# The four big projections by Strassen's seven block products, on eight cores of a Trainium2

## The chip, the cores and the metric

One program runs on all eight NeuronCores of a Trainium2 chip, each on its own 1024 tokens (four sequences of 2048, two cores to a sequence). The metric is the device time of the slowest core in microseconds. No core talks to another.

## The reference

One block of a streaming encoder, on activations of width 2048:

```python
h = rmsnorm(x, norm1_g)
b_a, c_a, v_a, v_b, g_a, g_b = split(h @ w_in)     # 1024 x4, 2048 x2 columns
u   = causal_depthwise_conv3(c_a * v_a)
y_a = (b_a * u) @ w_a_out
y_b = pool_scale * per_group_linear(trailing_mean(v_b, 2/4/8/16) - v_b)
x   = x + (sigmoid(g_a + b) * y_a + sigmoid(g_b + b) * y_b) @ w_o
h2  = rmsnorm(x, norm2_g)
x   = x + (silu(h2 @ w_gate) * (h2 @ w_up)) @ w_down   # width 5632
out = rmsnorm(x, final_g)
```

## The kernel before, in words

Five engines run one program text each; `Emitter.op` issues an instruction on its engine in program order and puts in front of it the semaphore waits that its tiles need. Nothing is reordered, so an instruction that waits holds all behind it on its engine.

Weights come from DRAM in f32 and are cast to bf16 on the way by POOL's queue, in jobs, into the four slots of `wring` (`issue_job`, L297 to L311). A slot's next job is issued when TensorE is done with it, so three jobs are always ahead. All matmuls go through `mm_group` (L406): a chain of 128x128 stationary blocks, each with 512 moving columns, into one PSUM bank.

- Start: nine row tiles of x are loaded by SP; for each, `norm_stats` (ScalarE Square and Sqrt, L367), `norm_to_T` (VectorE reciprocal and scaling L383, TensorE transposes L394, evacuation L399 or L402) give h transposed in `hT`. Tiles 5 to 8 are transposed in between the first groups of `mixA`. Matmuls on zeros (`warm`) keep TensorE busy meanwhile.
- Convolution branch, j = 0 to 7: 16 halo columns, then per half of the tokens (512 columns) three groups of 16 matmuls; `mixA_ew_blk` combines.
- Pooling branch, j = 0 to 7: two groups of 16; running sums L569, then L575.
- Gates, j = 0 to 15, per half: 16 + 8 + 16 + 2 matmuls into four banks; sigmoids L611 and L614, products L617, L619, L622, into `mg`.
- Output projection: 4 column blocks of 512 x 8 token tiles x 16 matmuls, added into the residual `x1`, which lies in SBUF in f32 (L665). In the last column block the second norm of tile i follows at once, and the transposed result takes the place of `mg`.
- FFN: 4 groups of 11 hidden blocks. Gate/up: per block and half 16 + 16 matmuls, Silu L694, product L696. Down: 4 column blocks x 8 token tiles x 11 matmuls, added into `x1` (L753). In the last group the final norm follows each tile (`final_norm`, L724), then SP stores it. The first gate/up group of the FFN runs on the first token half while the second half is still being normed.

Of the kernel before, what the change touches and what calls it, by code (L numbers as in the profile page):

```python
# [1 line left out]

# [5 lines left out]
F32 = mybir.dt.float32  # L8
# [6 lines left out]
D = 2048  # L15
KD = 16
T = 1024
# [5 lines left out]
G = 4  # L23
FG = NF // G
SLOT = 6144
NSLOT = 4
EPS = 1e-6
POOL_W = (2, 4, 8, 16)

JOB_SIZES = ([6144] * 8 + [6144, 6144, 4096] + [5376] * 16 + [4096] * 8  # L30
             + ([4096] * FG + [FG * 512] * 4) * G)
WTOTAL = sum(JOB_SIZES)

def pack_weights(inputs):
# [9 lines left out]
    def kv(a):  # L44
        return a.reshape(a.shape[0] // 128, 128, a.shape[1]).transpose(1, 0, 2)

    blocks = []
    for j in range(8):
        blocks.append(np.stack([kv(w_in[:, wi * 1024 + j * 128:wi * 1024 + (j + 1) * 128]) for wi in range(3)],
                               axis=1).reshape(128, -1))  # L50
    for q in range(3):
        n = 3 if q < 2 else 2
        blocks.append(kv(w_in[:, 3072 + q * 384:3072 + q * 384 + n * 128]).reshape(128, -1))
    for j in range(16):
        g = j // 4
        blocks.append(np.concatenate([
            np.stack([kv(w_in[:, 4096 + j * 128:4096 + (j + 1) * 128]),
                      kv(w_in[:, 6144 + j * 128:6144 + (j + 1) * 128])], axis=2).reshape(128, -1),
            kv(w_a_out[:, j * 128:(j + 1) * 128]).reshape(128, -1),
            kv(w_pool[g * 256:(g + 1) * 256, (j % 4) * 128:(j % 4 + 1) * 128]).reshape(128, -1)], axis=1))  # L60
    for db in range(4):
        for hh in range(2):
            blocks.append(kv(w_o[hh * 1024:(hh + 1) * 1024, db * 512:(db + 1) * 512]).reshape(128, -1))
    for gi in range(G):
        for fi in range(FG):
            fidx = gi * FG + fi
            blocks.append(np.concatenate([kv(w_gate[:, fidx * 128:(fidx + 1) * 128]).reshape(128, -1),
                                          kv(w_up[:, fidx * 128:(fidx + 1) * 128]).reshape(128, -1)], axis=1))
        for db in range(4):
            blocks.append(kv(w_down[gi * FG * 128:(gi + 1) * FG * 128, db * 512:(db + 1) * 512]).reshape(128, -1))  # L70
# [8 lines left out]
class Res:  # L79
    def __init__(self, name):  # L80
        self.name = name
        self.reset()
# [762 lines left out]
```

How the kernel before makes its waits and increments, by code:

```python
    def wait_tokens(self, engname, toks):  # L118
        if self.cur != engname:
            return
        need = {}
        for (s, v) in toks:
            if need.get(s, 0) < v:
                need[s] = v
        for s, v in need.items():
            if self.waited.get(s, 0) >= v:
                continue
            self.eng.wait_ge(s.h, v)
            self.waited[s] = v
# [1 line left out]
    def op(self, engname, fn, reads=(), writes=(), sem=None, inc=1):  # L131
        toks = []
        for r in reads:
            toks += r.w
        for w in writes:
            toks += w.w + w.r + w.pr
        self.wait_tokens(engname, toks)
        ins = fn(self.eng) if self.cur == engname else None
        s = sem if sem is not None else self.engsem[engname]
        s.count += inc
        if ins is not None:
            ins.then_inc(s.h, inc)
        tok = (s, s.count)
        for r in reads:
            r.r.append(tok)
        for w in writes:
            if w.r:
                w.pr = w.r
                w.r = []
                w.w = [tok]
            else:
                w.w.append(tok)
        return tok
```

## Time and profile before

| | |
|---|---|
| runs (three) | 1609.62, 1611.08, 1611.22 us; median 1611.08 |
| span of the profiled execution, slowest core | 1608.6 us (the page gives no other time for it); the cores 1606.4 to 1608.6 |
| mean granted TensorE clock by core | 0.991 to 0.994 |
| instructions | 19498 |
| busy | TensorE 1567.9, VectorE 396.1, ScalarE 211.5, POOL 51.8 us |
| HBM | 252.89 MB read, 8.39 MB written |

The span runs from a core's first to its last instruction; the runs' times hold 2.5 us more. PE stands for TensorE's matmuls, PEld for its weight loads, DVE for VectorE, ACT for ScalarE, POOL for GpSimd, SP for SyncE, with q for a queue; L696 is a line of the kernel. A row of windows has the stretch and its length, then busy time and instructions of PE, PEld, DVE, ACT, POOL, the granted clock as a share of 2.4 GHz, the busy share of the 16 DMA engines and GB/s. A busy TensorE isn't one at its peak, since its records overlap: the step from one matmul to the next has to be read from the starts of groups. POOL's 51.8 us are the issuing of DMAs.

### The profile page before, as it was taken

To read this page: it belongs to the slowest core of one execution; us is meant where nothing else is said; L and a number is where in the kernel's file an instruction comes from. 1 tells how busy PE (TensorE), PEld (TensorE's weight loads), DVE (VectorE), ACT (ScalarE), POOL (GpSimd) and SP (SyncE) were. 2 spreads that over 40 slices of the span, in tenths; PEclk is the share of its full clock that TensorE was granted. 3 is DMA by queue.
4 is the path that set the end of the run, shared out by engine and by line. 5 is a ranking of instruction groups with operands and counts; after the bars stand their busy time and mean duration, and the time that the engine had idled before them with its cause. 6 is when DMAs were issued, how large, how long until landed. Compare 5 with 4: busy or idle time off the path is not lost.

```text
span 1608.6 us, 19498 instructions; the slowest of 8 cores (1606.4 to 1608.6 us)
## 1 busy us (share of the span) xinstructions
PE 1567.9 (97%) x7655; PEld 725.1 (45%) x7805; DVE 396.1 (25%) x527; ACT 211.5 (13%) x330; POOL 51.8 (3%) x102
## 2 busy tenths in 40 slices
PE   5999999999999999999999999999999999999997
PEld 2444444444444444544444444444444444444443
DVE  4422236222222212621012211022111022110126
ACT  5311112111111100510000000000000000000004
POOL 0000000000000000000000000000000000000000
PEclk8999999999999999999999999999999999999999
DMA  9863325444454385374464344453444543444615
GB/s 264 157 119 66 67 49 85 81 76 69 71 84 79 53 239 102 53 131 78 73 102 73 56 79 74 84 92 53 79 79 73 94 83 53 79 77 73 103 24 209
DMA packets 18215, 146.14 MB, mean 91 GB/s; under 512 B 2160, under 2 KB 2240, under 8 KB 2624
## 3 DMA queue, kind: packets, MB, share of 16 engines
q0 software_dynamic: 13968, 116.40, 43.1%
q1 hardware_dynamic: 4160, 28.49, 5.1%
q8 instruction: 65, 1.06, 0.3%
q14 instruction: 22, 0.18, 0.0%
HBM read 252.89 MB, written 8.39 MB: 162 GB/s over the span
## 4 chain that ended last, share of the span: by engine, by line
PE 96%; DMA 2%; issue 1%; DVE 1%; ACT 1%; SPq 0%; POOL 0%; DVEq 0%; ACTq 0%; POOLq 0%
PE ps L409 95%; DMA wring<-wpack 1%; DMA arenaC<-x_c 1%; PE ps L394 1%; ACT arenaC L368 0%; DVE arenaC L383 0%; DVE arenaB L724 0%; ACT arenaA L399 0%; DVE arenaB L402 0%; DVE arenaA L402 0%; ACT L373 0%; SPq L418 0%; DVE arenaA L753 0%; DVE arenaA L665 0%; ACT arenaC L614 0%
## 5 line engine op out<-in xcount | busy, mean ns | idle before, releaser
L409 PE MATMUL ps<-arenaB,wring 128*128 128x512 bf16 x2759 | 605.6, 379 | 4.5 <-DVE arenaB L402 1.5
L409 PE MATMUL ps<-arenaA,wring 128*128 128x512 bf16 (+1 forms) x2700 | 520.7, 351 | 8.2 <-DMA wring<-wpack 4.5
L409 PEld LDWEIGHTS ps<-arenaB,wring 128*128 128x128 bf16 x2816 | 275.3, 98 | 333.5 <-issue 1.6
L409 PEld LDWEIGHTS ps<-arenaA,wring 128*128 128x128 bf16 x2752 | 241.6, 98 | 286.7 <-issue 9.2
L409 PE MATMUL ps<-wring,arenaC 128*128 128x512 bf16 x1380 | 303.1, 379 | 1.5
L409 PEld LDWEIGHTS ps<-wring,arenaC 128*128 128x128 bf16 x1408 | 137.7, 98 | 166.2
L696 DVE TENSOR_TENSOR arenaC<-ps,arenaC 128x512 bf16<-128x512 f32 x88 | 60.9, 692 | 541.5 <-PE ps L409 539.7
L694 ACT ACTIVATE arenaC<-ps 128x512 f32<-128x512 f32 x88 | 52.5, 597 | 772.9 <-PE ps L409 772.9
L753 DVE TENSOR_TENSOR arenaA<-ps,arenaA 128x512 f32<-128x512 f32 x128 | 88.5, 691 | 200.3 <-PE ps L409 193.5
L409 PE MATMUL ps<-wring,arenaB 128*128 128x512 bf16 x501 | 110.4, 379 | 0.6
L309 POOL DMA_DIRECT2D wring<-wpack x94 | 49.6, 529 | 1430.6 <-PE ps L409 1430.6
L409 PEld LDWEIGHTS ps<-wring,arenaB 128*128 128x128 bf16 x512 | 49.8, 98 | 59.3
L368 ACT ACTIVATE arenaC<-arenaA 128x2048 bf16<-128x2048 f32 x18 | 34.4, 1909 | 153.0 <-DVE arenaA L665 86.8
L619 DVE SCALAR_TENSOR_TENSOR arenaC<-ps,prm,arenaC 128x512 f32<-128x512 f32 x32 | 24.0, 751 | 108.9 <-ACT arenaC L614 108.5
L617 DVE TENSOR_TENSOR arenaC<-ps,arenaC 128x512 f32<-128x512 f32 x32 | 22.1, 691 | 103.5 <-PE ps L409 103.5
L614 ACT ACTIVATE arenaC<-ps,prm 128x512 f32<-128x512 f32 x32 | 22.0, 687 | 142.5 <-PE ps L409 142.5
L665 DVE TENSOR_TENSOR arenaA<-ps,arenaA 128x512 f32<-128x512 f32 x32 | 21.6, 689 | 75.1 <-DMA arenaA<-x_c 38.4
L611 ACT ACTIVATE arenaC<-ps,prm 128x512 f32<-128x512 f32 x32 | 22.0, 687 | 100.3 <-PE ps L409 100.3
L488 DVE TENSOR_TENSOR arenaC<-ps,arenaC 128x512 f32<-128x512 f32 x16 | 11.1, 692 | 93.2 <-PE ps L409 92.4
L569 DVE TENSOR_TENSOR arenaC<-arenaC 128x1039 f32<-128x1039 f32 (+3 forms) x20 | 24.8, 1238 | 26.8 <-ACT arenaC L561 25.5
L394 PE MATMUL ps<-identb,arenaC 128*128 128x128 bf16 (+1 forms) x272 | 17.9, 221 | 12.4 <-DVE arenaC L383 10.8
L495 DVE SCALAR_TENSOR_TENSOR arenaC<-arenaC,prm 128x512 f32<-128x512 f32 x32 | 24.0, 752 | 18.2 <-ACT arenaC L491 16.2
(48 smaller groups left out, 243.0 us busy)
## 6 DMA issues: line engine op xcount, KB each, us to landing
wring<-wpack POOLq DMA_DIRECT2D x53, 1024.0 KB, 9.6
wring<-wpack POOLq DMA_DIRECT2D x16, 1408.0 KB, 12.1
wring<-wpack POOLq DMA_DIRECT2D x16, 1344.0 KB, 11.9
wring<-wpack POOLq DMA_DIRECT2D x9, 1536.0 KB, 13.9
arenaA<-x_c SPq DMA_DIRECT2D x10, 1024.0 KB, 25.8
out<-arenaB SPq DMA_DIRECT2D x8, 1024.0 KB, 3.9
arenaB<-x_c SPq DMA_DIRECT2D x4, 1024.0 KB, 23.2
arenaC<-norm_g SPq DMA_DIRECT2D x2, 1024.0 KB, 13.4
```

Of the source, the lines that this page charges most:

```text
L309: em.op("pool", lambda e, s=s, sz=sz, off=off: e.dma_start(out=slot(s, sz), in_=wpack[:, off:off + sz]), writes=[r_slot[s]], sem=s_w[s], i ...
L368: em.op("act", lambda e: e.activation(out=sq[0:npart, :], in_=src_ap, func=AF.Square, accum_out=ssb[0:npart, col:col + 1]), reads=src_res, ...
L394: ins = e.transpose(pt[:, k, 0:npart], hbuf[0:npart, k * 128:(k + 1) * 128], identb[0:npart, 0:npart])
L409: ins = e.matmul(out_ap, lhs_fn(k), rhs_fn(k), start=(k == 0), stop=(k == nk - 1))
L495: em.op("dve", lambda e, sh=sh, pc=pc: e.scalar_tensor_tensor(out=R3[:, o0:o0 + 512], in0=R2[:, c0 - sh:c0 - sh + 512], scalar=PW(pc), in1 ...
L569: em.op("dve", lambda e, dst=dst, cur=cur, lo=lo, sh=sh: e.tensor_tensor(out=dst[:, lo:TT], in0=cur[:, lo:TT], in1=cur[:, lo - sh:TT - sh] ...
L611: em.op("act", lambda e, b0=b0, par=par, j=j: e.activation(out=sga[par], in_=bank(b0), func=AF.Sigmoid, bias=PW(j)), reads=[r_bank[b0], R[ ...
L617: em.op("dve", lambda e, b0=b0, par=par: e.tensor_tensor(out=m1, in0=bank(b0 + 1), in1=sga[par], op=ALU.mult), reads=[r_bank[b0 + 1], r_sg ...
L619: em.op("dve", lambda e, b0=b0, par=par, j=j: e.scalar_tensor_tensor(out=m2, in0=bank(b0 + 3), scalar=PW(64 + j), in1=sgb[par], op0=ALU.mu ...
L694: em.op("act", lambda e: e.activation(out=sg[par], in_=bank(bg), func=AF.Silu), reads=[r_bank[bg]], writes=[r_sg[par]])
L696: em.op("dve", lambda e: e.tensor_tensor(out=act[:, fi, o0:o0 + 512], in0=bank(bu_), in1=sg[par], op=ALU.mult), reads=[r_bank[bu_], r_sg[p ...
L753: em.op("dve", lambda e, b=b, i=i, db=db: e.tensor_tensor(out=x1[:, i, db * 512:(db + 1) * 512], in0=bank(b), in1=x1[:, i, db * 512:(db + ...
```

## The change

With X cut in four blocks along rows and contraction and W along contraction and columns, the product is built from seven block products in place of eight. The blocks of a unit are 1024 of the contraction by 128 weight columns by 512 tokens (projections with weights stationary), or 128 tokens by 512 columns (activations stationary: output and down projection). Five sums of weight blocks and five of activation blocks are used, all bf16 in SBUF, made by VectorE.

`run_group` emits the seven products one after another, with lists of follow-up work (`urg`, by product) and a queue of other VectorE work (`pump`) spread between; what belongs to the last product is handed on as `carry` and is emitted behind the next unit's first product. Banks X, Y, Z of two parities are used.

```diff
+            def run_group(prods, urg, carry, extra=None):
+                for s in range(7):
+                    prods[s]()
+                    if extra and s in extra:
+                        extra[s]()
+                    for c in (carry if s == 0 else urg.get(s - 1, [])):
+                        c()
+                    pump(-(-len(queue) // (7 - s)))
+                return urg.get(6, [])
...
+            def common(par, X, Y, Z, need_e=True):
+                urg = {
+                    0: [lambda: acopy(tS[par], bank(X), [r_bank[X]], [r_tS[par]])],
+                    1: [lambda: tt(tD[par], bank(Y), tS[par], ALU.subtract, [r_bank[Y], r_tS[par]], [r_tD[par]])],
+                    2: [lambda: tt(tE[par], bank(Z), tD[par], ALU.add, [r_bank[Z], r_tD[par]], [r_tE[par]])],
+                    3: [], 4: [lambda: tt(tE[par], tE[par], bank(Y), ALU.subtract, [r_tE[par], r_bank[Y]], [r_tE[par]])],
+                    5: [], 6: [],
+                }
+                return urg
...
+                spec = [(X, "s5", "22", True), (Y, "22", "s4", True), (Z, "s1", "s1", True), (X, "11", "s3", False),
+                        (Y, "s2", "11", False), (Z, "s7", "s7", False), (X, "s6", "s6", False)]
```

`c11` adds bank Z and tD after product 5, `c22` adds bank X and tE after product 6; C12 and C21 are read straight from banks X and Y. `prep_w` queues a unit's five weight sums (`ASPEC`: 1024 elements a partition each), `prep2` those of a gate/up unit or, for a down unit, five (chunk 0) or ten; both are called one unit ahead.

In-projection: 32 units of 4096 weight columns (two output blocks of 128 each): 8 of C and v (`cv`), 4 of B, 4 of v_b, 16 of gates. The first two `cv` are done plainly, with 16-matmul groups (`std_mm`), before the block sums of h are complete:

```diff
+            n1(5)
+            n1(6)
...
+            halo_mm(19, 2)
+            std_mm(19, "1", 0, 0)
+            std_mm(19, "2", 0, 1)
+            n1T(5, 2, "dve")
+            n1(7)
...
+            n1T(6, 3, "dve")
+            n1(8)
+            for s_ in range(1):
+                for spec in BSPEC:
+                    bsum(spec, 0, H4, H4, r_Hr, r_Hr)
+            halo_mm(20, 3)
+            n1T(7, 2, "dve")
+            n1T(8, 3, "dve")
...
+            halo_cv(2, 0)
+            std_ew(0, 0, 0, 1)
+            std_mm(20, "1", 0, 2)
```

(`n1` is statistics and scaling of a tile, `n1T` its transposes and evacuation, `bsum` a sum of 2048 elements.) Then the other 14 of the first 16 units follow, with the running sums of the pooling (`pool_tail`) and the convolution (`conv_tail`) put on the queue. In the gate units the 8 + 2 matmuls per half of the mixer of unit j - 1 stand behind products 1 to 4 of unit j.

Output projection: two halves of 1024 columns (dp), four groups (tp) of token tiles tp and tp + 4, products of 8 matmuls. The sums of W_o (`w_sum`, 4096 elements) and of merged (`mo_sum`, 1024) of the first group are emitted at the start:

```diff
+            mo_sum(AS["s5"], 0)
+            w_sum(BS["s4"], W0, r_w0, W0s, r_w0)
+            mo_sum(AS["s1"], 0)
+            w_sum(BS["s1"], W0, r_w0, W0s, r_w0)
+            for f_ in (lambda: w_sum(BS["s3"], W0, r_w0, W0s, r_w0), lambda: mo_sum(AS["s2"], 0),
+                       lambda: mo_sum(AS["s7"], 0), lambda: w_sum(BS["s7"], W0, r_w0, W0s, r_w0),
+                       lambda: mo_sum(AS["s6"], 0), lambda: w_sum(BS["s6"], W0, r_w0, W0s, r_w0)):
+                f_()
...
+                    if dp == 1:
+                        urg[6].append(lambda tp=tp: norm2_stage1(tp))
+                        if tp > 0:
+                            o = tp - 1
+                            extra = {3: lambda o=o: norm2_tr(o, o), 5: lambda o=o: norm2_tr(o, o + 4)}
+                            urg[0].append(lambda o=o: norm2_scale(o, o))
+                            urg[2].append(lambda o=o: norm2_scale(o, o + 4))
+                            for spec in BSPEC:
+                                urg[5].append(lambda o=o, spec=spec: norm2_sums(o, spec))
...
+            ffn_begin2()
+            prep2(units[0])
+            pump(100)
+            norm2_scale(3, 3)
+            norm2_tr(3, 3)
+            norm2_scale(3, 7)
+            norm2_tr(3, 7)
+            for spec in BSPEC:
+                norm2_sums(3, spec)
```

`norm2_stage1` also stores the residual to a DRAM scratch `x1_d` (SP, 16 stores of 0.5 MB), since its SBUF space goes to the FFN. FFN: chunks of 4, 8, 8, 8, 8, 8 hidden blocks, `CHUNKS`. Weight loads go through four slots; a down unit (one dp of one chunk, products of 2 or 4 matmuls, four groups) takes two of them:

```diff
+            for c in range(NCH):
+                if c + 1 < NCH:
+                    units.append(("ff", c + 1, 0))
+                for dp in range(2):
+                    units.append(("dn", c, dp))
+                if c + 1 < NCH:
+                    for f in range(1, CHUNKS[c + 1]):
+                        units.append(("ff", c + 1, f))
...
+                    b = raw2[n_ % 4]
+                    load(key, bb(b, JOFF[key][1]), r_slot[b], s_slot[12 + n_ % 4])
...
+                    carry = run_group(prods, urg, carry)
+                    issue2(1)
+                    continue
...
+                if ui in hostq:
+                    prep2(hostq[ui])
...
+                        urg[3].append(lambda X=X, i0=i0: acopy(st(i0)[:, 512:1024], bank(X), [r_bank[X]], [r_st[i0]]))
...
+                        def accum(i, t, dp=dp):
+                            return lambda: em.op("pool", lambda e: e.dma_start(
+                                out=x1_d[t * 128:(t + 1) * 128, dp * 1024:(dp + 1) * 1024],
+                                in_=fb(STB[i], 1024, (i % 2) * 1024), accum_op=ALU.add), reads=[r_st[i]],
+                                writes=[r_x1d[t][dp]], sem=s_st[i], inc=16)
+                        urg[5].append(accum(i0, t1))
+                        urg[6].append(accum(i1, t2))
...
+                    left = 4 - tp
+                    keep = list(queue)
+                    queue.clear()
+                    take = -(-len(keep) // left)
+                    queue.extend(keep[:take])
+                    rest = keep[take:]
+                    carry = run_group(prods, urg, carry)
+                    queue.extend(rest)
+                pump(100)
+                issue2(2)
```

So the down results of chunks 0 to 4 are staged in four SBUF buffers (`st`) and added to the scratch by DMAs from POOL's queue. For the last chunk the scratch is read back into SBUF by SP (16 loads of 0.5 MB), six additions per group go there (two of them on GpSimd), and in its second unit the final norms of tiles tp and tp + 4 are handed on in `carry` behind each group.

## Rows read from the trace of the kernel before

**Rows 1.** Page, busy time by engine, and the granted clock in 40 slices
```profile
PE 1567.9 (97%) x7655; PEld 725.1 (45%) x7805; DVE 396.1 (25%) x527; ACT 211.5 (13%) x330; POOL 51.8 (3%) x102
...
PEclk8999999999999999999999999999999999999999
```

**Rows 2.** Windows by stage: length, busy (count) by engine, PEclk, DMA share, GB/s
```profile
575.00:683.00 108.00, 106.52 (x558) 51.26 (x567) 37.73 (x46) 22.95 (x32) 3.51 (x7) 1.00 0.60 132
683.00:1572.00 889.00, 883.17 (x4054) 403.11 (x4135) 149.56 (x211) 63.35 (x101) 30.25 (x58) 1.00 0.45 77
1572.00:1598.10 26.10, 25.99 (x119) 11.63 (x119) 20.25 (x22) 12.96 (x24) 0.00 (x0) 1.00 0.51 210
1598.10:1608.60 10.50, 0.01 (x1) 0.00 (x0) 5.62 (x5) 2.40 (x4) 0.00 (x0) 0.67 0.68 279
...
60.00:100.00 40.00, 39.72 (x239) 18.98 (x243) 11.90 (x18) 5.35 (x9) 1.06 (x2) 1.00 0.98 175
```

**Rows 3.** Chain that ended last, gate stage: start us, us, what
```profile
369.23 10.74 PE ps L409 x49
...
509.52 10.75 PE ps L409 x49
```

**Rows 4.** Groups by line and form: busy us, mean ns of one
```profile
L753 DVE TENSOR_TENSOR arenaA<-ps,arenaA 128x512 f32<-128x512 f32 x128 | 88.5, 691 | 200.3 <-PE ps L409 193.5 <-remote 6.7
...
L694 ACT ACTIVATE arenaC<-ps 128x512 f32<-128x512 f32 x88 | 52.5, 597 | 772.9 <-PE ps L409 772.9
...
L368 ACT ACTIVATE arenaC<-arenaA 128x2048 bf16<-128x2048 f32 x18 | 34.4, 1909 | 153.0 <-DVE arenaA L665 86.8 <-DVE arenaA L753 46.3 <-DVE rstdb L378 19.4
...
L575 DVE SCALAR_TENSOR_TENSOR arenaA<-arenaC 128x1024 bf16<-128x1024 f32 x8 | 9.8, 1225 | 0.8
...
L402 DVE COPY arenaA<-ps 128x2048 bf16<-128x2048 bf16 x4 | 4.9, 1223 | 5.8 <-ACT arenaA L399 3.7 <-ACT arenaC L466 2.1
```

**Rows 5.** Timeline of VectorE in the pool stage: start us, us
```profile
253.80 3.92 DVE L569 TENSOR_TENSOR arenaC<-arenaC 128x1039 f32<-128x1039 f32 x3 [3.03 <-ACT arenaC L561]
257.83 1.23 DVE L575 SCALAR_TENSOR_TENSOR arenaA<-arenaC 128x1024 bf16<-128x1024 f32 x1
258.97 0.17 DVE L579 TENSOR_TENSOR tmp<-arenaC,inv_sb 128x16 f32<-128x16 f32 x1
```

**Rows 6.** Timeline of TensorE at the first projection matmuls
```profile
36.07 10.35 PE L409 MATMUL ps<-arenaA,wring 128*128 128x16 bf16 x63 [4.47 <-DMA wring<-wpack]
...
41.15 0.15 PEld L409 LDWEIGHTS ps<-arenaA,wring 128*128 128x128 bf16 x1 [0.28 <-issue]
...
41.57 0.15 PEld L409 LDWEIGHTS ps<-arenaA,wring 128*128 128x128 bf16 x1 [0.28 <-issue]
```

**Rows 7.** Timeline of the last stage
```profile
1580.07 1.91 ACT L368 ACTIVATE arenaC<-arenaA 128x2048 bf16<-128x2048 f32 x1 [2.17 <-DVE rstdb L378]
1580.15 2.35 DVE L724 SCALAR_TENSOR_TENSOR arenaB<-arenaA,rstdb,arenaC 128x2048 f32<-128x2048 f32 x1
```

**Rows 8.** Timeline of POOL's weight loads, one per convolution unit
```profile
66.26 0.53 POOL L309 DMA_DIRECT2D wring<-wpack  x1 [21.63 <-PE ps L409]
87.79 0.53 POOL L309 DMA_DIRECT2D wring<-wpack  x1 [21.00 <-PE ps L409]
```

**Rows 9.** DMA: queue shares, and issues with us to landing
```profile
q0 software_dynamic: 13968, 116.40, 43.1%
q1 hardware_dynamic: 4160, 28.49, 5.1%
...
wring<-wpack POOLq DMA_DIRECT2D x53, 1024.0 KB, 9.6
...
out<-arenaB SPq DMA_DIRECT2D x8, 1024.0 KB, 3.9
```

**Rows 10.** Waits: us in total, times, longest
```profile
POOL wring L309 <- PE ps L409: 1430.6, 87, 32.2
```

More of the change, by code:

```diff
@@ L1 @@
 from contextlib import ExitStack
+from collections import deque
 import numpy as np
@@ L15 @@
 D = 2048
-KD = 16
 T = 1024
@@ L406, in mm_group @@
-            def mm_group(e, out_ap, lhs_fn, rhs_fn, nk):
-                ins = None
-                for k in range(nk):
-                    ins = e.matmul(out_ap, lhs_fn(k), rhs_fn(k), start=(k == 0), stop=(k == nk - 1))
-                return ins
-            PW = lambda c: prm[:, c:c + 1]
-            xsem = s_x + s_r[0:6]
+                em.op("pe", f, reads=[R["identb"], R["warm"]], writes=[r_bank[7]])
             for ti in range(NTOK + 1):
@@ new lines, in program, with issue1, issue_mix @@
+            order1 += [("gate", j) for j in range(16)]
+            issued = {"n": 0}
+            def issue1():
+                n = issued["n"]
+                if n >= len(order1):
+                    return
+                issued["n"] = n + 1
+                b = raw1[n % 3]
+                load(order1[n], bb(b), r_slot[b], s_slot[n % 3])
+            def issue_mix(j):
+                if j < 16:
+                    if j < 2:
+                        em.hand(r_ex[j], r_hb + [R["sq"], R["c12s"]] + r_R2 + r_R3)
+                    load(("mix", j), exb[j % 2], r_ex[j % 2], s_ex[j % 2])
@@ new lines, in halo_mm, with f @@
+            def halo_mm(b, B):
+                q = quadv(b)
+                def f(e):
+                    ins = None
+                    for n_, (x0, x1_) in enumerate((("11", "12"), ("21", "22"))):
+                        for k in range(16):
+                            w = q[x0 if k < 8 else x1_]
+                            ins = e.matmul(bank(B)[:, 16 * n_:16 * n_ + 16], w[:, k % 8, :], hTh[:, k, :],
+                                           start=(k == 0), stop=(k == 15))
+                    return ins
+                em.op("pe", f, reads=[r_slot[b], R["halo"]], writes=[r_bank[B]])
@@ new lines, in program @@
+            for c in carry:
+                c()
+            carry = []
+            for pe, ew in pend:
+                pe()
+                ew()
+            for i in range(4):
+                for t in (i, i + 4):
+                    em.hand(r_xa[t], [R["bu"], R["pl"]])
+                    em.op("sp", lambda e, i=i, t=t: e.dma_start(
+                        out=fb(i, 1024, (t // 4) * 1024), in_=x_c[H + t * 128:H + (t + 1) * 128, 0:1024]),
+                        writes=[r_xa[t]], sem=s_xa[t], inc=16)
@@ L783, in _, with res_cache @@
+            for c in carry:
+                c()
+            em.wait_tokens("sp", [t for r_ in r_out for t in r_.w])
+            em.wait_tokens("pool", [t for r_ in r_x1d for q in r_ for t in q.w])
+        cache = {}
+        def res_cache(nm):
+            if nm not in cache:
+                cache[nm] = em.resource(nm)
+            return cache[nm]
+        hbsq = fb(17, 1024).bitcast(BF16)
+        s_xs2 = [dsem() for _ in range(NTOK)]
         @block.sync
```

1464 lines of the change are left out of this document (917 added, 547 removed).

## The prediction

> **What bounds the kernel now.** I read the page first: TensorE is busy 97% of the span, and its granted clock is 9 tenths or more in all slices but the first [rows 1]. No other engine is above 25%. The windows by stage say where that holds: in the FFN (683 to 1572 us) TensorE is busy 883 of 889 us at clock 1.00, VectorE 150 and ScalarE 63 [rows 2]. So no wait ends late; the stream of matmuls itself sets the end. Its step comes from the chain of waits: between 369.23 and 509.52 us there are 13 pieces of 50 matmuls (49 in the record and the one that follows), so one 128x512 matmul costs (509.52 - 369.23) / 13 / 50 = 0.2158 us [rows 3]. The program issues 7104 of them: 7104 x 0.2158 = 1533 us of the 1608.6 us span. The other 75.6 us are the norm at the start, transposes, halo columns and the tail.
>
> **What the change removes.** A Strassen unit has 7 products of 8 matmuls where there were 64: 56. In-projection: 30 of 32 units, 240 matmuls fewer; output projection 64; gate/up 44 x 8 = 352; down 22 x 8 = 176. Sum 832 x 0.2158 = 179.5 us. If nothing else moved: 1429 us.
>
> **What it adds.** Every unit now also costs VectorE work: the sums of the weight blocks, and the combination of products out of PSUM. Prices: a 128x512 f32 operation 0.69 us, 1024 elements 1.23 us [rows 4]; followed by an independent operation the step is 0.09 less (257.83 to 258.97 is 1.14 for a 1.23 one), followed by one that needs its result 0.08 more (three take 3.92) [rows 5]. So about 0.60 to 0.78 for 512 f32; I use 0.62 on average, 0.69 for one that has waited.
>
> The trace has no bf16 tensor_tensor with both inputs in SBUF. The bounds: the 1024-element f32 output, 1.23 us, above; the 2048-element bf16 copy, 1.22 us [rows 4], below, which is two elements a cycle, so 1024 elements take 0.69 and step by 0.60 us. I take the lower, its rows being bf16 on both sides. The Trainium skill ("VectorE: DVE Perf Modes", section on the perf-mode tier table) gives tensor_tensor on bf16 in SBUF 2x; on f32 or PSUM 1x. The f32 rows agree, the bf16 half no run here shows; by it the sum below stays as it is.
>
> *FFN gate/up, 44 units.* TensorE 56 x 0.2158 = 12.09 us. VectorE: seven f32 operations 4.3, five weight sums 3.0, half of five 512-element activation sums 0.9: 8.2 us. But VectorE must also be in time: product 4 overwrites bank Y and waits for tD, due after 4 x 1.73 = 6.9 us; carry, activation sums, two weight sums and tD end at 5.7. Hidden. 531.7 us, plus 3 for a cold clock at the start (below).
>
> *In-projection.* The start: TensorE's first projection matmuls still begin at 36.07 [rows 6] and end at 46.4. Now the transposes of tiles 5 to 8 stand behind them, and VectorE does in order evacuation, scaling (2.35 each [rows 7]), evacuation, scaling, five 2048-element sums (1.13 each, 5.7), two evacuations: 47.4 + 1.2 + 2.35 + 1.2 + 2.35 + 5.7 + 2.4 = 62.6 us. Until then bank 2 isn't free, and after the gap the clock is cold: matmuls come 0.42 apart [rows 6], about 6 us of them. The six remaining plain groups end at 86.4, the two convolution tails and the first sum at 94. So the first Strassen product starts at 94. Then 14 units x 12.09 = 169, halo columns: a unit of 96 matmuls and 32 halo ones took 21.53 [rows 8], so 0.81 per 32, 8 us for ten. Pool tails of 6 to 14 us run on VectorE in the unit after; double-buffered banks take most, I count 7 us of stalls. To 278. Gates: 16 x 12.09 + 15 x 20 x 0.2158 = 258; VectorE has 11 of 16.4 us. To 536.
>
> *Output projection and second norm.* The block sums of merged and of W_o can't begin before the last gate is merged (their space holds h). Counted from the last gate product: four mixer matmul groups, each waiting for the evacuation before it, leave merged complete at 6.7; five pairs of sums (1024 elements 0.60, 4096 elements 2.2) 14.0; two queued sums 1.2; tD 0.7. So product 4 starts at 22.6, and with products 4 to 6 the first tile group ends at 27.8 (unhindered 12.1 + 4.3). Three more groups 36.3 + 1.8. The second half adds scaling (four of 1.14), evacuations and five sums per group, and its reciprocal waits for ScalarE (Square over 2048 1.91 [rows 4]): one cycle is 18 us of VectorE order where TensorE needs 14.2. After the last group TensorE needs both token halves complete (every product sums blocks of both), so it idles some 17 us; before, the first gate group ran on the first half meanwhile. Counted from the second half's start: the last addition from bank Z is done at 11 in the first group, then 15, 18 and 18 us later, 62; from there in VectorE's order sums and addition 3.7, statistics 2.4, five weight sums 3.0, scaling 2.3, transposes 1.1, evacuation 0.7, scaling 2.3, transposes 1.1, evacuation 1.1: first FFN product at 79.7. Together 27.8 + 38.1 + 79.7 = 145.6, to 682.
>
> *Down, chunks 0 to 4.* TensorE 1008 x 0.2158 = 217.5 us. Here the ring is short. Load n is issued when unit n - 4 frees its slot, but a down unit takes two slots; so the load for the gate/up unit behind a pair of down units is issued as the first of them ends, and its sums are queued on VectorE in the second, before tD. A load lands 9.6 us after issue [rows 9]; with the additions to the scratch ahead of it I put 12.9. VectorE stands, then sum, sum, tD: product 4 starts 12.9 + 2 instead of 3.45 us in, a stall of 11.4. The second raw block of that second down unit was issued 5.2 us before the first starts, 4.4 late: stall 2.9. A full chunk loses 14 us, four 57. Before, a load had an idle queue and POOL waited 1430.6 us for TensorE, never the other way [rows 10]. Chunk 0 (products of 2 matmuls, 3.02 us a group) is bound by VectorE at 4.05 us a group, 8 us, and by the stall: 20 in all. Sum 217.5 + 77 = 294.5, to 1511 (with the 3).
>
> *The additions to DRAM*: 16 of 0.5 MB per chunk. None in the trace. Below: by bytes sent like the output store, 28.49 MB in 5.1% of the span, 2.9 us per MB [rows 9], 1.45 each. Above: by the weight load, 116.4 MB in 43.1%, 6.0 us per MB, 3.0 each; the window 60 to 100 us with the engines 98% busy at 175 GB/s says the same [rows 2, 9]. I take 2.9, since each also reads what it adds to: 46 us in a full pair of down units of 63, beside 18 of loads: full, not over. At 1.45 the total is 14 us less. The Trainium skill ("Collectives: The Full Stack", the bandwidth ceiling) has a transfer with an add at half the rate of a copy, because it reads two sources; by it the figure stays 2.9; no run here shows it.
>
> *Last chunk and tail.* 48.3 of TensorE; dp = 0 loses 5.5. In dp = 1 two final norms stand on VectorE between a group and the next tD (reciprocal waits for ScalarE's 1.91, scaling 2.35 [rows 4, 7]): 12 us a cycle against 6.04, three times 6. Tail 13 against 10.5 now [rows 2]. To 1511 + 48.3 + 23.5 + 13.3 = 1596.
>
> The sum is a span; before, the span is 1608.6 and the runs' median 1611.1, 2.5 more. **Forecast 1599 us**, 0.7% under. Other unknowns of this account (start, norm, ring) are each good for 5 to 10 us either way: 1570 to 1630 if this case holds. 0.2% (3 us) is about what a measurement can tell from no change.
>
> **Rivals.**
> 1. *Account as above*: 0.60. For it: [rows 2] VectorE is 17% busy, so hidden work has room; against: many terms. Faster 0.38, same 0.06, slower 0.16.
> 2. *The waits for loads are hidden* (a load lands before VectorE comes to it, no queue before it): the 57 + 12 vanish, 1599 - 69 = 1530 to 1545. Against: issue to landing is 9.6 with an idle queue [rows 9]. 0.18, all faster.
> 3. *The additions bind* (other side, slower): from 3.4 us each the queue, 16 x 3.4 + 18 = 72, outlasts the pair of down units with their stalls; four buffers then hold ScalarE, bank X and product 6. At 4 us each: 82 for 63, 4 x 19.5 + 20 more: 1697; at 5: 1780. Against: 3.0 upper price. For: reading and writing back the same DRAM rows is in no row. 0.14.
> 4. *bf16 sums at one element a cycle*: 8 (start), 24 (gate/up; 11.5 of 12.09 us, late at tD), 33 (units with ten sums), 34 (output), 20 (rest): 1720. Against: the bf16 copy. 0.05.
> 5. *No gain because products are as costly as groups*: start-up of 8-matmul groups. [rows 3] show no gap at group ends; 0.03, 1650 at 0.2 us a group more.
>
> Range: 0.1 above rival 3's middle and 4, 0.05 below 2: 1530 to 1690. Faster 0.38 + 0.18 = 0.56, same 0.07, slower 0.37.
>
> **What would show it.** Matmuls of 128x512 6272 x 0.2158; first Strassen product near 94 us, first FFN product near 682. In full chunks' second down unit one VectorE wait of about 11 us for a load, TensorE idle with it. If such waits fall on product 4 through tD, the step is right. Scratch additions landing over 10 us after issue and ScalarE waiting for them mean rival 3. A weight sum lasting 0.69 us rules rival 4 out. The forecast is wrong first of all if the loads' lead or the price of an addition is.

## The result and the profile after

The changed kernel takes 1844.8 us against 1610.4 us, a ratio of 1.1455 with a 95% interval of 1.1423 to 1.1487. Some executions of every kernel are disturbed, with the cores of one die at a lower clock, so all times here are medians of the undisturbed ones (1840.7 and 1849.0 us for the changed kernel; over all five the median is 1851.4). The forecast was 1599 us with a range to 1690: wrong in size and in sign.

The page of the kernel after (busy time, the granted clock and the DMA share in 40 slices, DMA queues, the costliest group of matmuls, DMA issues with their time to landing):

```profile
PE 1499.7 (81%) x6969; PEld 658.2 (36%) x6969; DVE 1127.5 (61%) x1712; ACT 322.6 (17%) x545; POOL 157.0 (8%) x225
...
PEclk8799999999999896966999789979997889889996
DMA  9444445655559663289956996599849994899564
...
q0 software_dynamic: 29376, 158.35, 61.5%
...
L396 PE MATMUL ps<-arena 128*128 128x512 bf16 x6272 | 1455.5, 394 | 281.9 <-DVE arena L383 196.7
...
arena<-wpack POOLq DMA_DIRECT2D x104, 1024.0 KB, 11.7
x_scratch<-arena POOLq DMA_DIRECT2D x80, 512.0 KB, 16.8
```

The 832 products are gone (6272 are left), and TensorE is busy 68 us less than in [rows 1], not 179: it waits 282 us, and the granted clock is lower in most of the slices where it does. (PEclk and DMA are in tenths, so 9 can be full.) The slices tell the place: from the 18th on, the DMA row stands at 8 or 9 in groups of two or three slices, and the clock and TensorE dip in the same ones. The windows give that in numbers (length, TensorE busy with its count, clock, DMA share, GB/s):

```profile
722.00:1847.00 1125.00, 872.40 (x3696) 0.88 0.78 112
900.00:1000.00 100.00, 94.20 (x425) 0.97 0.64 101
1000.00:1100.00 100.00, 61.30 (x250) 0.83 1.02 111
1100.00:1200.00 100.00, 97.94 (x442) 0.98 0.65 103
800.00:900.00 100.00, 49.31 (x160) 0.67 1.03 109
```

The stretches of gate and up units (900, 1100) run well; those that hold down units (800, 1000) have the DMA engines full (a share of 1.02 and 1.03), at some 110 GB/s, and TensorE busy for 49 and 61 of 100 us. The waits of the kernel after (engine and line, what ended the wait, us in total, times, the longest):

```profile
PE ps L396 <- DVE arena L383: 196.7, 52, 22.6
ACT arena L386 <- DMA x_scratch<-arena: 188.8, 47, 7.0
DVE arena L383 <- DMA arena<-wpack: 137.1, 13, 21.1
...
PE ps L396 <- ACT arena L386: 79.0, 34, 5.0
```

Neither DMA wait has a counterpart in [rows 10], where POOL waited for TensorE. L386 is the copy of a product from PSUM into a staging buffer `st`, and it waits until the addition from that buffer has landed: 47 times. One down unit shows both waits together, first on TensorE, then on VectorE (timelines: start, duration, operation, idle time before it and what ended it):

```profile
1010.64 1.02 PE L396 MATMUL ps<-arena 128*128 128x512 bf16 x4 [3.31 <-ACT arena L386]
1012.93 9.12 PE L396 MATMUL ps<-arena 128*128 128x512 bf16 x28 [1.26 <-DVE arena L383]
1042.19 13.34 PE L396 MATMUL ps<-arena 128*128 128x512 bf16 x52 [20.14 <-DVE arena L383]
```

```profile
1018.82 0.69 DVE L383 TENSOR_TENSOR arena<-ps,arena 128x512 f32<-128x512 f32 x1 [1.03 <-ACT arena L386]
1039.94 1.29 DVE L383 TENSOR_TENSOR arena<-arena 128x1024 bf16<-128x1024 bf16 x2 [20.43 <-DMA arena<-wpack]
```

VectorE comes to a block sum at 1019.5, and the load lands at 1039.9. Behind that sum stands the addition that frees the bank of product 4, so TensorE idles 20.14 us: it is the stall that the prediction put at 11.4 us. The last 28 matmuls before the gap take 9.12 us, 0.33 each where 0.2158 is full speed; the mean clock over them is 0.67.

Of the prediction's times ahead of the FFN, the first came as forecast, the end of the gates came 7 us late, and the start of the FFN 40 us late. First Strassen product, and first FFN product, on TensorE:

```profile
92.88 7.49 PE L396 MATMUL ps<-arena 128*128 128x512 bf16 x24 [8.49 <-DVE arena L383]
```

```profile
722.58 42.74 PE L396 MATMUL ps<-arena 128*128 128x512 bf16 x191 [1.25 <-ACT arena L386]
```

92.9 us against 94; 722.6 us against 682. (The end of the gates is in the account below.)

### The profile page after: what moved, and what is told of

It is laid out like the page before. It is cut to its first block, busy times and chain, and to the rows that moved or that the text cites. A ratio compares the mean times of both kernels' runs of the same rounds, so it can differ in the third digit from the quotient of the medians.

```text
span 1847.4 us, 21242 instructions; the slowest of 8 cores (1721.3 to 1847.4 us)
## 1 busy us (share of the span) xinstructions
PE 1499.7 (81%) x6969; PEld 658.2 (36%) x6969; DVE 1127.5 (61%) x1712; ACT 322.6 (17%) x545; POOL 157.0 (8%) x225
## 4 chain that ended last, share of the span: by engine, by line
PE 54%; DMA 25%; DVE 11%; issue 6%; ACT 2%; POOL 1%; SPq 0%; DVEq 0%; POOLq 0%; ACTq 0%
PE ps L396 53%; DMA arena<-wpack 12%; DMA x_scratch<-arena 12%; DVE arena L383 9%; DVE arena L489 1%; DMA arena<-x_c 1%; ACT arena L471 1%; ACT arena L386 1%; PE ps L1011 1%; POOL arena L383 1%; PE ps L656 0%; DVE arena L644 0%; DVEq L169 0%; DVE arena L749 0%; SPq L1191 0%
## 5 line engine op out<-in xcount | busy, mean ns | idle before, releaser
L396 PE MATMUL ps<-arena 128*128 128x512 bf16 x6272 | 1455.5, 394 | 281.9 <-DVE arena L383 196.7
L396 PEld LDWEIGHTS ps<-arena 128*128 128x128 bf16 x6272 | 621.1, 101 | 1107.4 <-issue 448.7
L383 DVE TENSOR_TENSOR arena<-ps,arena 128x512 f32<-128x512 f32 (+1 forms) x624 | 426.4, 688 | 380.5 <-PE ps L396 257.2
L383 DVE TENSOR_TENSOR arena<-arena 128x1024 bf16<-128x1024 bf16 (+5 forms) x732 | 492.4, 704 | 151.7 <-DMA arena<-wpack 137.1
L386 ACT COPY arena<-ps 128x512 f32<-128x512 f32 (+3 forms) x246 | 144.4, 596 | 777.4 <-PE ps L396 407.0
L390 POOL DMA_DIRECT2D arena<-wpack x124 | 68.7, 570 | 1200.7 <-DVE arena L383 733.7
L383 DVE TENSOR_TENSOR arena<-arena,ps 128x512 f32<-128x512 f32 x130 | 89.0, 685 | 89.7 <-PE ps L396 89.7
L1341 POOL DMA_DIRECT2D x_scratch<-arena x80 | 70.0, 876 | 409.9 <-DVE arena L383 381.9
L489 DVE SCALAR_TENSOR_TENSOR arena<-arena,rstdb 128x1024 bf16<-128x1024 f32 (+3 forms) x33 | 60.0, 1832 | 18.1 <-DMA x_scratch<-arena 16.1
L471 ACT ACTIVATE arena<-arena 128x2048 bf16<-128x2048 f32 (+2 forms) x33 | 49.2, 1492 | 48.5 <-DVE arena L383 40.4
## 6 DMA issues: line engine op xcount, KB each, us to landing
x_scratch<-arena POOLq DMA_DIRECT2D x80, 512.0 KB, 16.8
```

Of the source, the lines that this page charges most:

```text
L383: em.op(eng, lambda e: e.tensor_tensor(out=out, in0=a, in1=b, op=op), reads, writes)
L386: em.op("act", lambda e: e.copy(out=out, in_=a), reads, writes)
L390: em.op("pool", lambda e: e.dma_start(out=dst, in_=wpack[:, off:off + n]), writes=[r], sem=sem, inc=16)
L396: ins = e.matmul(out, lhs(k), rhs(k), start=(start and k == 0), stop=(k == n - 1), skip_group_check=True)
L471: act(lambda e, ap=ap, q=q: e.activation(out=sq[0:npart, 0:ap.shape[1]], in_=ap, func=AF.Square, accum_out=ssb[0:npart, col + 32 * q:col + ...
L489: dve(lambda e: e.scalar_tensor_tensor(out=dst, in0=src, scalar=rstdb[0:npart, col:col + 1], in1=gain, op0=ALU.mult, op1=ALU.mult), rr + [ ...
```

## Experiments

Two theories of the FFN stood at the start. **A**: the additions to the scratch cost far more of the 16 DMA engines than the 2.9 us I took, so that in a pair of down units the engines are full and every transfer is late. **B**: the DMA engines are not the cause; the loads are issued too late for VectorE's queue, and the additions only wait in it.

**Plain writes in place of additions, and no transfers at all.** Both edits leave the engines' work as it is.

```diff
# e1_plain_write
-                                in_=fb(STB[i], 1024, (i % 2) * 1024), accum_op=ALU.add), reads=[r_st[i]],
+                                in_=fb(STB[i], 1024, (i % 2) * 1024)), reads=[r_st[i]],
# e2_no_add_dma
-                        urg[5].append(accum(i0, t1))
-                        urg[6].append(accum(i1, t2))
```

> The 80 transfers from the staging buffers to the DRAM scratch write instead of adding (so the results of chunks 0 to 4 and the residual are left out of the output); same bytes from SBUF, same queue, same waits. Theory A (an addition keeps the 16 DMA engines about 5.4 us, 432 of the software queue's 1136 us over 80 transfers, and this fills the queue in the down units): the transfers fall to about 1.5 us each, ScalarE's 189 us of waits for them vanish, the load behind a down pair lands about 11 instead of 20 us late, the time falls by 110 to 150 us to 1700 to 1740. Theory B (the late issue of the load behind a down pair is the bulk of the loss, whatever is in the queue): 1800 or more.

> The 80 transfers are gone altogether (results of chunks 0 to 4 left out). Theory A: 10 to 20 us below the run with plain writes, about 1690 to 1720; VectorE's wait for the load behind each down pair stays at 8 to 10 us, because that load is still issued with no lead. Theory B: the same 1800 as there.

Measured: plain writes 1672.6 us (ratio 1.0389, 1.0373 to 1.0405), none 1642.4 us (1.0207, 1.0184 to 1.0229). The same bytes in the same places, without the addition, give back 172 us; leaving them out gives 30 more. Both are more than A gave (110 to 150, and 10 to 20). The page and the waits with plain writes, then without any:

```profile
q0 software_dynamic: 29376, 158.35, 52.9%
...
x_scratch<-arena POOLq DMA_DIRECT2D x80, 512.0 KB, 5.2
...
PE ps L396 <- DVE arena L383: 119.8, 39, 15.6
DVE arena L383 <- DMA arena<-wpack: 68.1, 8, 14.0
```

```profile
q0 software_dynamic: 17856, 116.40, 39.9%
...
PE ps L396 <- DVE arena L383: 92.5, 40, 9.8
DVE arena L383 <- DMA arena<-wpack: 38.7, 7, 8.3
```

The share of q0 gives the price. It took 0.615 x 1847.4 = 1136 us of the 16 engines with additions, 0.529 x 1671.0 = 884 us with plain writes, 0.399 x 1641.1 = 655 us without: a plain write costs (884 - 655) / 80 = 2.9 us, an addition (1136 - 655) / 80 = 6.0 us. These are differences of the whole queue: what an addition does to the loads beside it is in them. ScalarE's wait for a staging buffer, 189 us, is 1.3 us with plain writes. A stands, B is down to what remains without additions.

**The block sums handed out later.** The order alone is changed: no sums of the next unit in the first two groups of a down unit, so that VectorE comes to them when the load has had more time.

```diff
-                    take = -(-len(keep) // left)
+                    take = -(-len(keep) // left) if tp >= 2 else 0
```

> In a down unit the weight sums of the next unit are queued for the third and fourth tile group alone, so VectorE comes to its wait for the load some 12 us later; same transfers, same arithmetic. Theory A: the queue needs 16 x 5.4 + 18 = 104 us for a pair of down units whatever VectorE does, so the pair stays at about 90 us and ScalarE's waits grow; gain under 30 us. Theory B: the stalls of about 20 us per pair go, 80 to 100 us faster.

Measured: 1815 us (1803.6 and 1827.2; ratio 1.1276, 1.1176 to 1.1376), 29 us less than the changed kernel, give or take some 16. That is A's "under 30", and far from the 80 to 100 of B. Its waits:

```profile
ACT arena L386 <- DMA x_scratch<-arena: 293.1, 55, 24.5
PE ps L396 <- ACT arena L386: 157.0, 38, 21.5
PE ps L396 <- DVE arena L383: 82.4, 49, 8.5
...
DVE arena L383 <- DMA arena<-wpack: 21.3, 6, 6.2
```

The wait for loads went from 137 to 21 us, as meant, and the wait for staging buffers rose from 189 to 293 us, with TensorE behind ScalarE in place of VectorE. A full queue gives that: most of the time is owed to its total, and the order chooses who waits. Against B.

**Half of the additions.**

```diff
                         urg[5].append(accum(i0, t1))
-                        urg[6].append(accum(i1, t2))
```

> The changed kernel with one of the two accumulating transfers of each pair of token blocks left out: 40 of 80 (half of what the down projection adds to the residual is left out of the output, and the sums for it are still made). Without any of them the kernel took 1642 us, with all 80 it took 1851 us. If each transfer costs its share wherever it falls (linear), this gives 1642 + 105 = 1747 us. If the price only counts once the DMA engines are full, the queue decides: measured by themselves among weight loads, an accumulation costs 5.7 us of the 16 engines and a load 6.5 us, and in the down part 32 loads in some 280 us with 40 additions in place of 80 ask for 208 + 228 = 436 us less than they did, so that most of the excess goes: 1660 to 1700 us. Theory A, in its strict form (a full queue), expects 1660 to 1700; linear would be 1747; above 1790 would say that a single late transfer per group, not the queue's load, sets the time.

Measured: 1693.8 us (ratio 1.0516, 1.0499 to 1.0534). From 0 to 40 additions 51 us, from 40 to 80 another 151 us. The time does not grow in proportion to the number: the first half fits mostly beside the loads, the second does not. In its trace (core 2) ScalarE waits 12 us for staging buffers, where it was 189 with all 80.

**The price by itself.** Blocks of transfers from POOL's queue, each block awaited before the next; nothing else runs.

```diff
+            for i in range(16):
+                em.op("pool", lambda e, i=i: e.dma_start(out=x1_d[reg(i)], in_=st[i % 8][:, reg(i)[1]],
+                                                         accum_op=ALU.add),
+                      writes=[r_d[i]], sem=sem16[i], inc=16)
+            allw(r_d)
...
```

Ahead of this block stands the same without `accum_op`; behind it come four additions and four plain writes one at a time, eight additions of 1 MB, twelve loads, twelve loads with eight additions between them, and a last transfer to `out`.

> Leaves out the whole computation: only transfers are issued, all from GpSimd's queue, in blocks one after the other, to measure the prices that the theory takes from the changed kernel as a difference. From that difference one accumulating transfer of 512 KB costs 5.4 us of the 16 DMA engines ((0.615 x 1847 us - 118.3 MB at 5.95 us per MB) / 80), while the plain residual store of the same 512 KB is taken at 1.5 to 1.6 us. Theory A (the accumulation itself is dear on the DMA engines): the block of 16 plain writes ends in 24 to 35 us, the block of 16 accumulating writes in 80 to 95 us, that is 5 to 6 us each against 1.5 to 2.2; one accumulating transfer alone takes 7 to 10 us against 4 to 5 for a plain one; an accumulation of 1 MB (2048 columns) costs twice one of 512 KB, 10 to 12 us, so the price goes by bytes. Rival B (the accumulation is cheap by itself and is dear only among the casting weight loads of the same queue): 16 accumulating writes end in under 50 us, and 12 loads with 8 accumulations between them take over 40 us more than 12 loads alone. Under A that difference is 8 x 5.4 = 43 us minus nothing as well, so the verdict rests on the block of accumulations alone.

Measured, in the timeline of POOL, which issues a block when the one before has landed (a row of several issues ends early; the next row's start is the block's end):

```profile
30.30 8.52 POOL L395 DMA_DIRECT2D x_scratch<-arena  x16 [29.60 <-DMA arena<-x_c]
67.64 14.07 POOL L399 DMA_DIRECT2D x_scratch<-arena  x16 [28.82 <-DMA x_scratch<-arena]
137.84 0.85 POOL L404 DMA_DIRECT2D x_scratch<-arena  x1 [56.13 <-DMA x_scratch<-arena]
144.61 0.85 POOL L404 DMA_DIRECT2D x_scratch<-arena  x1 [5.92 <-DMA x_scratch<-arena]
...
165.45 0.56 POOL L409 DMA_DIRECT2D x_scratch<-arena  x1 [5.96 <-DMA x_scratch<-arena]
168.93 0.55 POOL L409 DMA_DIRECT2D x_scratch<-arena  x1 [2.92 <-DMA x_scratch<-arena]
...
179.17 7.03 POOL L413 DMA_DIRECT2D x_scratch<-arena  x8 [2.87 <-DMA x_scratch<-arena]
233.98 6.40 POOL L418 DMA_DIRECT2D arena<-wpack  x12 [47.77 <-DMA x_scratch<-arena]
312.10 0.54 POOL L422 DMA_DIRECT2D arena<-wpack  x1 [71.72 <-DMA arena<-wpack]
...
435.69 0.54 POOL L429 DMA_DIRECT2D out<-x_scratch  x1 [109.90 <-issue]
```

Sixteen plain writes of 512 KB: 67.64 - 30.30 = 37.3 us, 2.33 each. Sixteen additions: 137.84 - 67.64 = 70.2 us, 4.39 each. Among loads: twelve loads alone take 312.10 - 233.98 = 78.1 us (6.5 each), with eight additions between them 123.6 us, so an addition costs 45.5 / 8 = 5.7 us. The expectation of 80 to 95 us for the block was too high, rival B's under 50 too low; the plain block (24 to 35 expected) was dearer, and an addition alone (7 to 10) and one of 1 MB (10 to 12; (233.98 - 179.17) / 8 = 6.9 measured) were cheaper. An addition is 1.9 times a plain write by itself, and 1.3 us dearer still beside loads. The 6.0 of the kernel is nearest to the figure among loads.

The Trainium skill ("Collectives: The Full Stack", the bandwidth ceiling) has a transfer with an add at half the rate of a copy, since it has two sources to read; the ratio 4.39 / 2.33 = 1.88 agrees, though the page speaks of another kind of transfer.

**The stage between gates and FFN.** Here the theories were **S**: scaling in place (L489) waits for the stores of the same rows to the scratch, and **O**: VectorE's and ScalarE's own order is longer than I counted. One such wait, on VectorE in the changed kernel:

```profile
694.72 1.28 DVE L489 SCALAR_TENSOR_TENSOR arena<-arena,rstdb 128x1024 bf16<-128x1024 f32 x1 [7.00 <-DMA x_scratch<-arena]
```

The first try removed the 16 stores and filled the scratch from x by one DRAM-to-DRAM transfer during the gates:

```diff
# e4_no_store, beside the 16 stores left out
+            em.op("sp", lambda e: e.dma_start(out=x1_d[:, :], in_=x_c[H:H + T, :]), reads=[R["pl"]],
+                  writes=[q for r_ in r_x1d for q in r_], sem=s_xs[0], inc=16)
# e6_no_store_no_add: the same transfer at the fifth unit of the FFN, and
-                        urg[5].append(accum(i0, t1))
-                        urg[6].append(accum(i1, t2))
```

> The 16 stores of the residual to the scratch during the output projection are left out; the scratch is filled with x by one transfer in the gate stage (so the output projection is missing in the residual). Theory: the scaling of the second norm writes in place over the rows that are being stored, so VectorE waits for each store (8.5 us seen), and the first gate/up product comes 43 us later than forecast for this; without the stores it comes 20 to 35 us earlier (at 690 to 700 us) and the total falls by as much. Rival: ScalarE's statistics and VectorE's own load set that stage; then under 8 us.

> The changed kernel without its 80 additions to the scratch and without the 16 stores of the residual into it during the second norm; the scratch is filled by one transfer from x that is issued at the fifth unit of the FFN, after the second norm, so that nothing of it lies in the stage between the gates and the FFN (what attention and the down projection add to the residual is left out of the output for all but the last chunk). Without the additions alone the kernel took 1642 us and its first FFN product came 174 us after the gates' last. Theory S (the second norm scales the residual in place and so waits for the stores, which share the DMA engines with the loads): the stage becomes 15 to 25 us shorter, first FFN product near 700 us, 1620 us in all. Theory O (the stage is late by VectorE's and ScalarE's own order of evictions, sums and scalings): first FFN product stays within 5 us of 722 us, 1637 to 1645 us. The forecast of the stage (682 us) would need 40 us.

The first gave 1816 us (ratio 1.128, 1.1255 to 1.1304), but was no clean test: the transfer delayed the gates themselves, where VectorE waited 32.1 us for a load and TensorE 29.1 us for VectorE, so that the last products of the gates came 32 us later. The stage behind them was 155 us long in place of 174. The second is cleaner: 1628.8 us (ratio 1.0132, 1.0097 to 1.0167) against 1642.4 with the stores. TensorE in it:

```profile
648.85 3.51 PE L396 MATMUL ps<-arena 128*128 128x512 bf16 x8 [2.96 <-ACT arena L386]
...
669.09 3.45 PE L396 MATMUL ps<-arena 128*128 128x512 bf16 x8 [2.96 <-ACT arena L386]
...
700.00 1.86 PE L1007 MATMUL ps<-identb,arena 128*128 128x128 bf16 x16 [18.86 <-DVE arena L489]
...
708.59 4.42 PE L396 MATMUL ps<-arena 128*128 128x512 bf16 x10 [1.25 <-ACT arena L386]
```

The first FFN product comes at 708.6, where it came at 721.5 with the stores and without additions, and the time falls by 14. One of these 13 us lies in the gates, which ended earlier; the stage itself is 162 us in place of 174. That is between S (15 to 25 us shorter) and O (under 5). It is also less than in the first try, and the trace shows a reason: VectorE waits 5.2 us for a weight load ahead of its last sums (until 694.15), where in the first try it waited for none. So S explains at least 12 of the 40 us. The gates had ended 7 us late (below). The other 21 no run took away; some 5 of them are that load in this run, the rest is VectorE's and ScalarE's order: a cycle of the second half is 669.09 - 648.85 = 20.2 us (I had 18), and after the last group TensorE idles 18.9, 3.6 and 1.3 us before and between the scalings.

**Strassen where SBUF holds everything.** The input projection and 43 of 44 gate and up units by Strassen; the output and down projections plain, with the residual resident in SBUF, as in the kernel before. No scratch, no store, no addition.

```diff
-        for dp in range(2):
-            jobs += [(("dn", c, dp, h), 512 * CHUNKS[c]) for h in range(2)]
+        jobs += [(("dn", c, db), 512 * CHUNKS[c]) for db in range(4)]
...
-                        urg[5].append(accum(i0, t1))
-                        urg[6].append(accum(i1, t2))
...
+            def dn_add(db, i, B):
+                v = x1(i)[:, db * 512:(db + 1) * 512]
+                tt(v, bank(B), v, ALU.add, [r_bank[B], r_x1[i]], [r_x1[i]])
```

> Strassen only where no DRAM is needed for it: the input projection (30 units of the changed kernel) and 43 of the 44 gate and up units stay Strassen products, the output projection and the down projection are plain as in the kernel before, and the residual stays resident in SBUF, so there is no DRAM scratch, no residual store and no accumulation. 832 - 248 = 584 products fewer than before: 6520 in place of 7104 of 512 columns. Theory A (the loss came from the accumulating and storing transfers and the down units' sums behind late loads): the first part as in the changed kernel (gates end at about 541 us), output projection and norm2 as in the kernel before (about 125 us), first FFN product at about 666 us, then (43 x 56 + 64 + 1024 in the gate, up and down parts) 3850 products x 0.2158 us = 831 us, tail 10 us: 1507 us span, and 1500 to 1545 us with what norm2 and the first block of hidden channels may cost; faster than the kernel before by 4 to 7%. Rival C (Strassen's own parts cost more than the products saved, VectorE's sums and evictions binding wherever the units are): gate and up units stall by several us each, 1580 us or more, no gain. Told apart by the TensorE share in the FFN stretch: A 94% and over, C under 90%.

(The FFN's products were miscounted there: 43 x 56 + 64 + 1408 of the down part = 3880, 837 us, which makes the sum 1513.) Measured: **1530.6 us**, ratio 0.9503 (0.9487 to 0.9519), faster than both kernels. Its page and its windows for output projection and norm, and for the FFN:

```profile
PE 1462.3 (96%) x7217; PEld 672.3 (44%) x7217; DVE 916.2 (60%) x1321; ACT 239.7 (16%) x380; POOL 66.0 (4%) x129
...
PEclk7789999999999999999999999999999999999998
...
541.00:676.00 135.00, 131.09 (x692) 1.00 0.53 131
676.00:1520.00 844.00, 833.62 (x3865) 1.00 0.45 86
```

TensorE is busy 834 of 844 us of the FFN at full clock, with VectorE at 60% of the span: Strassen's sums hide behind products of 8 matmuls when no DMA holds them up. (The run doesn't show this of the output and down projections, which are plain in it.)

**The input projection alone.** The same with the gate and up units plain again:

```diff
-                prods = wprods(b, pcof[("ff", f)], X, Y, Z, h2v, rmv2)
+                for half in range(2):
+                    plain_pe(b, half, o + 2 * half, o + 2 * half + 1)
+                    plain_ew(half, o + 2 * half, o + 2 * half + 1, f)
```

> Strassen in the input projection alone (240 products of 512 columns fewer than the kernel before), everything else plain with the residual resident: the faster version of the last batch with its 43 gate and up units made plain again, so that their 344 products come back. At 0.2158 us each that is 74 us more than 1532: 1606 us if the gate and up units saved all their products (theory A: the units that touch only SBUF give back their products in full, and what is missing is lost in the first stage, where the clock falls and the sums of x stand ahead). Since the first part was measured 34 us earlier in the gates' end than in the kernel before, the other sum is 1611 - 34 = 1577 us. Rival C (gate and up units with VectorE's sums save only about half of their products): 1577 us. Rival D: the hybrid's output projection and norm2 lose some 20 to 30 us against the kernel before, then 1600 us and over. The stage's times tell C from D: the first FFN product at about 668 us in both, and the FFN's TensorE share.

Measured: 1601.5 us, ratio 0.994 (0.992 to 0.996). By the two ratios the gate and up units give back (0.9940 - 0.9503) x 1610 = 70 us, give or take 4, of the 74 that their 344 products are worth. Rival D is out: from the first product of the output projection to the first FFN product behind the last transposes both kernels take 127 us (550.9 to 678.5, and 565.9 to 693.2 before).

The input projection gives 10 of 52, and the traces show where the rest goes. Its first Strassen product waits until 92 us; by then 168 products of 512 columns have started, against 248 in the kernel before, and 80 x 0.2158 = 17 us are lost. The gates' first sigmoid comes at 289.7 us for 279.7, 10 us late, though 112 products (24 us) fewer stood ahead of it: another 17 us went between. The gates themselves give back 25 of the 28 us that their 128 products are worth, since the output projection starts 15 us early, and some 5 us are lost behind it.

## Why the prediction was wrong

The step that failed is the price of an addition to DRAM. I put it at 2.9 us of the 16 engines, between bounds of 1.45 and 3.0 from an output store and a weight load [rows 9]. A plain write to the scratch does cost 2.9 us. An addition costs 6.0, twice the upper bound, because I bounded a read-modify-write with rows that only move data. The doubling itself was right (1.88 by itself, 2.1 in the kernel); it was the base that was wrong: I doubled the 1.45 us of an output store on SP's queue, where a plain write from POOL's queue takes 2.33 us by itself and 2.9 in the kernel. The output store has rows of 8 KB and the write rows of 4 KB, and which of the two, queue or rows, makes the difference no run shows. (512 KB are 0.524 MB, so the two bounds were 1.5 and 3.1; that changes nothing.) The prediction's own threshold was 3.4 us, so rival 3 (chance 0.14) is what happened, by its signs too: additions landing 16.8 us after issue, ScalarE waiting for them. With plain writes, at the price that I took, ScalarE waits 1.3 us: full, not over, as I had it for that price. Rival 3's row for 5 us each, 1780 us, and 40 us of late FFN start give 1820; at 5.7 us, a further 0.7 x 83 = 58 us, 1878, and at 6.0 us 1903. Measured 1845: its slope of 83 us for each us of price is too steep.

The price is not all of it. With plain writes the kernel still takes 1672.6 us, and without any transfer 1642.4: 3.9% and 2.1% slower than before. So at my own price the forecast would have been 74 us too low, and wrong in sign.

The difference of 246 us, by the runs:

- The additions, 202 us (1844.8 to 1642.4), where the forecast held 28 (twice the 14 us that it put on 1.45 us of price): 174 too little. In the FFN, from 722 us to the end, it is 1125 us against 919 without additions. TensorE is busy 872.4 against 829.7 of them for the same 3696 matmuls, so 163 us of the 206 are waits and 43 are slower matmuls. Most of the 43 is the clock: it stood at 0.50 (1.2 GHz) for 125 us of TensorE's busy time against 47 us, and half of the difference, 39 us, is lost.
- The stage before the FFN, 40 us: 12 or more for stores whose rows are overwritten in place, a wait the prediction didn't have (it priced the stores at nothing), 7 from the gates, and up to 21 for VectorE's and ScalarE's order. The prediction had allowed the norm 5 to 10 us.
- The remaining 32 us are load waits and clock that are there without any addition. The row of its FFN, with the clock at 0.95 where the forecast counted one cold stretch of 3 us, and two of its gaps:

```profile
722.00:1641.00 919.00, 829.74 (x3696) 0.95 0.45 91
...
923.87 8.87 PE L396 MATMUL ps<-arena 128*128 128x512 bf16 x40 [1.07 <-DVE arena L383]
...
966.66 33.70 PE L396 MATMUL ps<-arena 128*128 128x512 bf16 x146 [7.73 <-DVE arena L383]
```

3696 x 0.2158 = 797.6 us at full speed, so the matmuls take 32 us more; 23 of these are the 47 us at 0.50, the other 9 no run explains. A long gap is paid a second time in slower matmuls: behind the one of 7.73 us the clock is 0.50 from 966.66 to 970 and 1.00 from 972 on. Behind the one of 1.07 us it is 1.00 at once.

What was right: the bound of the kernel before and the 0.2158 us; the start (92.9 for 94) and the step of the gates. Their first sigmoid stands behind four products of 1.73 us, and ScalarE begins its table load at 289.0, so they began at 282 where 278 was forecast. One unit took (535.6 - 290.3) / 15 = 16.35 us, for 16.4. Behind the last sigmoid at 535.6 the unit has 34 more matmuls, 7.3 us, so they ended near 543, for 536:

```profile
L875 ACT ACTIVATE arena<-ps,prm x16: 687/687/687, 290.3 to 535.6; 128x512 f32<-128x512 f32 x16
L875 ACT ACT_TABLE_LOAD  x1: 1283/1283/1283, 289.0 to 289.0; - x1
```

The stall on product 4 behind a late load is there in place and manner. Rival 4 is out: a weight sum of 1024 bf16 elements takes 0.68 us, a step of 0.60. The group of such sums, with its shape:

```profile
L383 DVE TENSOR_TENSOR arena<-arena 128x1024 bf16<-128x1024 bf16 x520 | 338.7, 682 | 137.0 <-DMA arena<-wpack 136.7 <-issue 0.3
```

The Trainium skill ("VectorE: DVE Perf Modes", the perf-mode tier table) gives such an operation 2x, 1224 ns for 2048 elements, and the traces agree: ten of 2048 elements take 1216 ns on average. Rival 5 is out as well: the gate and up units return 70 of 74 us in the version with a resident residual. (Its 1650 us doesn't follow from its words: there are 982 groups for 528 before, so 0.2 us each on the 454 more would be 91 us and some 1690.) Rival 2 is out: without any addition VectorE still waits 38.7 us for loads.

Two things stay open: how the up to 21 us of the stage divide between VectorE's order, ScalarE's and late loads, and why an addition among loads costs 1.3 us more than one by itself.

## What to carry to other kernels

Saving matmuls was worth its arithmetic (70 of 74 us) where sums and results stayed on chip, and not where they left it; ask first what must leave SBUF to make room, and price that traffic in engine time, with the loads that it stands beside. A transfer that computes is not bounded by transfers that only move: measure it; here it cost twice the plain transfer of the same size from the same queue. Where the sum is near full (here 64 of 63 us at 2.9 us each), let the case where it is over have the larger chance. A queue that is full yields little to reordering: moving the sums moved the wait from one engine to the other.

## What the runs showed of the hardware

- An accumulating DMA of 512 KB f32 into DRAM: 4.39 us, a plain one 2.33 us; one at a time, 6.8 and 3.5 us from one issue to the next. Among casting weight loads 5.7 us.
- In transfers of 1 MB, with 8 KB to a row in place of 4 KB, eight additions took 233.98 - 179.17 = 54.8 us: 3.4 us for 512 KB, so the price is not by bytes alone.
- TensorE's mean granted clock in stretches of 100 us of the changed kernel was 0.67 and 0.83 where gaps of up to 20 us stood between the matmuls, a mixture of 0.50 and 1.00, and 0.97 and 0.98 in the others. It was 0.50 for about 4 us behind a gap of 7.73 us and stayed at 1.00 behind one of 1.07 us.
- A DRAM-to-DRAM transfer of 8 MB during the gates delayed them by 32 us, though TensorE was busy 255.7 of 258 us there without it: VectorE waited 32.1 us for one weight load.
